# Block products for the remaining projection pairs of a hybrid encoder layer, with a shorter weight ring and the decay work rearranged

## The chip, the cores and the metric

The kernel runs on one core of one Trainium2 chip, as one launch. The metric is the device time in microseconds (us). Three runs of the kernel before took 1218.38, 1219.05 and 1219.12 us, median 1219.05.

## The reference

One encoder layer on 256 tokens of width 1024, all in float32 (products by leading sizes):

```python
def token_mixer(h, ...):
    proj = h @ w_in                                   # (256,1024) @ (1024, 6176)
    z, xbc, dt_f, dt_b, q, k, v, gates = jnp.split(proj, SPLITS, axis=-1)
    xbc = jax.nn.silu(depthwise_conv(xbc, conv_w, conv_b))
    dtf, dtb = softplus(dt_f + dt_bias_f), softplus(dt_b + dt_bias_b)
    y = y_f + y_b + xs * d_skip                       # two SSD scans, 16 heads of 64, 2 groups
    y = rmsnorm(y * jax.nn.silu(z), g_ssm)
    br_ssm = y @ w_br_ssm
    q, k = rope(rmsnorm(q)), rope(rmsnorm(k))         # 8 query heads, 2 key/value heads of 128
    br_attn = blocked_attention(q, k, v) @ w_br_attn
    g_s, g_a = jnp.split(jax.nn.sigmoid(gates), 2, axis=-1)
    return (g_s * br_ssm + g_a * br_attn) @ w_out

x = x + token_mixer(rmsnorm(x, g_mix), ...)
x = x + moe_ffn(rmsnorm(x, g_ffn), ...)               # top 4 of 32 experts, each 1024x2048 and 1024x1024
return rmsnorm(x, g_final)
```

In the scan a head's weight for output token l and input token s is exp(a_l - a_s) times dt_s times (C_l . B_s) for s <= l in the forward direction, and mirrored in the backward one, with a the running sum of dt times A.

## The kernel before, in words

The mixer reads its weights as 36 "units" of 1024 rows by 256 columns (1 MB each): 6 for x, B and C (U_XBC), 4 for z (U_Z), key (U_K), 4 query (U_Q), value (U_V), 8 gates (U_G), 4 of w_br_attn (U_BA), 4 of w_br_ssm (U_BS), 4 of w_out (U_O). They pass through a ring of `RING_MIX` = 10 slots of SBUF: SyncE (SP) loads unit n when unit n - 10 is done (`unit_done`), in order of n, and behind certain units stand the loads of the running sums for the decay (`load_seg`). The rest of the ring's space, `over`, holds other things of the mixer (gates, xbc, z, q and k). Afterwards the whole space is a ring of 8 pairs of slots for the experts' weights (402.7 MB in all), of which 22 MB can be loaded ahead. `PAIR_ORDER` and `first_free` say in which order these pairs come free.

On TensorE a unit is 16 products of 128x256 (each is two rows of the trace, float32). The four query units are done as two pairs in another way, `query_pair`: the two units are the halves of a 2x2 block matrix, the tokens and the inner dimension are halved too, and seven block products of four products each take the place of eight (Strassen's scheme in Winograd's form). VectorE makes the sums of weights (`pair_sum_t1` to `t4`, 128x1024 each) and of rows; ScalarE copies three partial sums out of PSUM (`pair_parts`); VectorE adds four quarters of the result. An output of such a pair has its tokens on the partitions; gate and branch units before the change have their channels on the partitions (`unit(n, rhs=...)`).

The loop `for g in range(8)` is the head stage. Group g is two scan heads and one attention head: TensorE does gate unit g, the transposes of the attention weights (L716), the scores of head g+1 (L700), the scan's product (L729) and the attention output (L739). VectorE makes the masked exponents of the decay (`seg_mask`), the maxima of the scores, the scan's output and its gate by z (L1655, L1658), the softmax's scaling (L1637, L1639) and the weights (`seg_weight`, which multiplies by dt and by C.B). ScalarE takes the exponentials. Each engine works through its own queue in the order written; semaphores join the queues. Behind the head stage come the branch units, the sum of the two gated branches, w_out, the router, and then 32 experts, which read the stream of weights.

Of the kernel before, what the change touches and what calls it, by code (L numbers as in the profile page):

```python
# [40 lines left out]
PICKED = -2e38  # L41

UW = 256
UNIT = KD * UW
RING_MIX = 10
# [3 lines left out]
PAIR_ORDER = (7, 3, 4, 0, 6, 5, 1, 2)  # L49
# [10 lines left out]
U_XBC, U_Z, U_K, U_Q, U_V, U_G, U_BA, U_BS, U_O = 0, 6, 10, 11, 15, 16, 24, 28, 32  # L60
N_MIX = 36

# [40 lines left out]
def encoder_layer(nc, x, g_mix, w_in, conv_w, conv_b, dt_bias_f, dt_bias_b, a_log_f, a_log_b, d_skip,  # L103
                  g_ssm, q_norm_g, k_norm_g, w_br_ssm, w_br_attn, w_out, g_ffn, w_router, b_router,
                  w_mlp1, b_mlp1, w_mlp2, b_mlp2, g_final, consts, out):
    with ExitStack() as ctx:
# [15 lines left out]
        def sem(name):  # L122
# [6 lines left out]
        over = sb("over", [P, (RING - RING_MIX) * UNIT], at=place_of["ring"] + RING_MIX * UNIT * 4)  # L129
        sig = over[:, 0:4096].rearrange("p (m l) -> p m l", m=16)  # L130
        roped = over[:, 0:2560].rearrange("p (t n) -> p t n", t=TT)
# [3 lines left out]
        qk = over[:, 9216:11776].rearrange("p (t n) -> p t n", t=TT)  # L135
        kT = over[:, 11776:12288].rearrange("p (h l) -> p h l", h=KVH)

# [23 lines left out]
        stat = sb("stat", [P, 64])  # L161

# [3 lines left out]
        rB = arena[:, 2048:2304]  # L166
# [6 lines left out]
        ebuf = arena[:, 4880:6416].rearrange("p (h l) -> p h l", h=2)  # L173
        ropeb = arena[:, 4880:5392].rearrange("p (t n) -> p t n", t=TT)
        gbuf = arena[:, 6416:8464].rearrange("p (b h i l) -> p b h i l", b=2, h=2, i=TT)
        sum_a = [a.rearrange("p (k l) -> p k l", k=KD // 2) for a in
                 (arena[:, 5392:5904], arena[:, 5904:6416], arena[:, 8976:9488], arena[:, 8464:8976])]
        sum_w = [[a.rearrange("p (k l) -> p k l", k=KD // 2) for a in part] for part in
                 ((arena[:, 0:1024], arena[:, 1024:2048], arena[:, 6416:7440]),
                  (arena[:, 7440:8464], arena[:, 1024:2048], arena[:, 6416:7440]))]  # L180
        part_a, part_b = rB, sqb
# [54 lines left out]
        def x_quarter(t, half):  # L236
            return hT[:, half * (KD // 2):(half + 1) * (KD // 2), t * P:(t + 1) * P]
# [15 lines left out]
        act_step = sem("act_step"); dve_step = sem("dve_step"); pool_step = sem("pool_step")  # L253
# [12 lines left out]
        sums_ready = sem("sums_ready"); prod_psum = sem("prod_psum"); first_taken = sem("first_taken"); quarter_ready = sem("quarter_ready")  # L266
        qsq_ready = sem("qsq_ready"); qr_ready = sem("qr_ready"); roped_ready = sem("roped_ready")
        qT_psum = sem("qT_psum"); qT_ready = sem("qT_ready")
        seg_masked = sem("seg_masked"); seg_exp = sem("seg_exp"); g_ready = sem("g_ready")
# [5 lines left out]
        yr_ready = sem("yr_ready"); rB_psum = sem("rB_psum")  # L275
        ssq_psum = sem("ssq_psum"); ssq_ready = sem("ssq_ready"); rB_ready = sem("rB_ready")
# [59 lines left out]
        def mix_src(n):  # L336
# [6 lines left out]
            if n < U_V:  # L343
                return cols(w_in[0], Q0 + (n - U_Q) * UW)
            if n == U_V:
                return cols(w_in[0], Q0 + AH * AD + KVH * AD)
            if n < U_BA:
                return cols(w_in[0], G0 + (n - U_G) * UW)
# [64 lines left out]
        def _(sp):  # L413
# [12 lines left out]
            for n in range(N_MIX):  # L426
# [7 lines left out]
                if U_G + RING_MIX <= n < U_G + RING_MIX + 6:  # L434
                    g = n - U_G - RING_MIX + 2
                    sp.wait_ge(seg_masked, 2 * g - 2)
                    if g == 3:
                        sp.wait_ge(roped_ready, 5)
                    load_seg(g)

            def first_free(p):
                if 2 * p < RING_MIX:
                    sp.wait_ge(unit_done, max(n for n in range(N_MIX) if mix_slot(n) == 2 * p + 1) + 1)
                elif p == 7:
                    sp.wait_ge(sc_psum, AH)
                    sp.wait_ge(roped_ready, 5)
                    sp.wait_ge(seg_masked, NH)
                    sp.wait_ge(yz_ready, 2 * KD)
                elif p == 6:
                    sp.wait_ge(cb_psum, 2)  # L450
                    sp.wait_ge(yz_ready, 2 * KD)
                    sp.wait_ge(unit_done, U_O)
                    sp.wait_ge(yg_ready, KD)
                else:
                    sp.wait_ge(mix_ready, 4)
# [1456 lines left out]
```

## Time and profile before

| | us |
|---|---|
| median of three runs | 1219.05 |
| profiled execution: its span, first to last instruction | 1218.8 |
| TensorE busy in it | 1178.1 |
| VectorE busy | 375.4 |
| ScalarE busy | 194.2 |
| GpSimd busy | 23.3 |

The times of the runs and the span of the profiled execution differ by 0.25 us; what lies around the span is within that. The page gives one execution: busy times, the span in 40 slices, and the chain that ended last. The rows further down are lines of that page and of the trace. Neighbouring instructions of one engine overlap a little in the trace (the end of one is recorded after the next has begun), so that the distance between two starts says what an instruction costs in a full queue, and its duration what it costs when someone waits for its end.

### The profile page before, as it was taken

Reading aid. Unit: us, or ns where it says so; the run is one execution under the profiler, and the core shown is the slowest. Engines: PE = TensorE matmul, PEld = TensorE weight load, DVE = VectorE, ACT = ScalarE, POOL = GpSimd, SP = SyncE. Lnnn points to the kernel's source line nnn. Section 1 sums busy time; section 2 is a strip of 40 time slices with the busy share of each in tenths; the row PEclk is TensorE's granted clock in tenths of the full one; section 3 lists DMA queues with packets and bytes.
Section 4 is the critical chain, followed back from the end, with each engine's and each line's share of the span. In section 5 each row is a group of like instructions: output and inputs, shape, how many; then the busy total and the mean of one; then the engine's idle time right before and its main releaser. Section 6 shows DMA issues by size and latency. Waiting matters only on the chain.

```text
span 1218.8 us, 14634 instructions
## 1 busy us (share of the span) xinstructions
PE 1178.1 (97%) x5561; PEld 561.1 (46%) x5561; DVE 375.4 (31%) x1034; ACT 194.2 (16%) x404; POOL 23.3 (2%) x36
## 2 busy tenths in 40 slices
PE   8999999999999999999999999999999999999996
PEld 7888888887433333333333333333333333333332
DVE  4537997122322222322222222222222222222212
ACT  2122344001111111111111111111111111111112
POOL 0001111000000000000000000000000000000000
PEclk9999999999999999999999999999999999999998
DMA  9945543667899999999999999999999999999995
GB/s 306 330 138 156 170 152 133 262 251 296 322 423 427 428 429 428 427 429 425 429 428 427 429 429 430 426 429 429 429 429 426 429 429 429 427 428 427 429 426 240
DMA packets 71479, 448.98 MB, mean 368 GB/s; under 512 B 6536, under 2 KB 44044, under 8 KB 45837
## 3 DMA queue, kind: packets, MB, share of 16 engines
q1 hardware_dynamic: 68186, 446.85, 89.5%
q10 hardware_dynamic: 3251, 1.54, 0.5%
q8 instruction: 30, 0.49, 0.2%
q14 instruction: 12, 0.10, 0.0%
HBM read 447.29 MB, written 1.08 MB: 368 GB/s over the span
## 4 chain that ended last, share of the span: by engine, by line
PE 76%; DMA 20%; ACT 2%; DVE 1%; issue 1%; POOL 0%; ACTq 0%; SPq 0%; DVEq 0%
PE bank L898 41%; DMA ring<-in_w_mlp_dram 19%; PE bank L580 14%; PE bank L893 4%; PE bank L873 4%; PE bank L583 2%; PE bank L882 1%; PE bank L937 1%; ACT arena L1319 1%; PE bank L644 1%; PE bank L729 1%; PE bank L556 1%; PE bank L887 1%; PE bank L739 1%; PE bank L805 1%
## 5 line engine op out<-in xcount | busy, mean ns | idle before, releaser
L898 PE MATMUL bank<-ring,arena 128*64 128x512 f32 x2928 | 654.8, 595 | 20.4 <-DMA ring<-in_w_mlp_dram 19.8
L898 PEld LDWEIGHTS bank<-ring,arena 128*64 128x64 f32 x2928 | 202.0, 137 | 417.4 <-issue 372.2
L1813 DVE TENSOR_TENSOR arena<-bank,b1T 128x256 f32<-128x256 f32 x126 | 53.1, 421 | 467.0 <-PE bank L937 463.9
L580 PE MATMUL bank<-hT,ring 128*128 128x256 f32 x544 | 119.6, 379 | 0.0
L580 PEld LDWEIGHTS bank<-hT,ring 128*128 128x128 f32 x544 | 103.1, 190 | 14.3 <-issue 0.4
L1316 ACT ACTIVATE arena<-bank 128x512 f32<-128x512 f32 x32 | 19.1, 597 | 404.9 <-PE bank L898 404.9
L1799 DVE TENSOR_TENSOR arena<-bank,prmT 128x512 f32<-128x512 f32 x30 | 20.8, 692 | 181.7 <-PE bank L882 181.7
L893 PE MATMUL bank<-arena 64*128 64x512 f32 x256 | 63.6, 615 | 0.8 <-ACT arena L1366 0.8
L873 PE MATMUL bank<-xres,arena 128*64 128x512 f32 x248 | 60.0, 604 | 0.0
L937 PE MATMUL bank<-cst,arena 128*128 128x128 f32 x256 | 42.0, 286 | 6.3 <-ACT arena L1319 6.3
L937 PEld LDWEIGHTS bank<-cst,arena 128*128 128x128 f32 x256 | 26.8, 140 | 39.9 <-ACT arena L1316 26.0
L1326 ACT ACTIVATE arena<-arena 128x256 f32<-128x256 f32 x64 | 26.7, 417 | 89.4 <-DVE arena L1815 89.4
L1349 ACT ACTIVATE arena<-bank 128x512 f32<-128x512 f32 x30 | 17.9, 597 | 123.6 <-PE bank L898 123.6
L873 PEld LDWEIGHTS bank<-xres,arena 128*64 128x64 f32 x248 | 15.1, 136 | 40.4 <-issue 40.4
L893 PEld LDWEIGHTS bank<-arena 64*128 64x128 f32 x256 | 22.0, 186 | 23.2 <-issue 21.6
L882 PEld LDWEIGHTS bank<-cst,arena 128*128 128x128 f32 x124 | 17.2, 207 | 25.2 <-issue 25.2
L583 PE MATMUL bank<-ring,hT 128*128 128x256 f32 x128 | 28.3, 379 | 0.0
L580 PE MATMUL bank<-arena,ring 128*128 128x256 f32 x128 | 28.2, 380 | 0.0
L580 PE MATMUL bank<-over,ring 128*128 128x256 f32 x128 | 27.8, 379 | 0.0
L1818 DVE SCALAR_TENSOR_TENSOR arena<-arena 128x256 f32<-128x256 f32 x62 | 26.4, 425 | 2.1
L1820 DVE TENSOR_TENSOR arena<-arena 128x256 f32<-128x256 f32 x62 | 26.3, 425 | 2.1
L1347 ACT ACTIVATE arena<-bank 128x256 f32<-128x256 f32 x30 | 11.5, 384 | 95.1 <-PE bank L887 95.1
(268 smaller groups left out, 803.7 us busy)
## 6 DMA issues: line engine op xcount, KB each, us to landing
ring<-in_w_mlp_dram SPq DMA_DIRECT2D x184, 2048.0 KB, 29.5
ring<-in_w_in_dram SPq DMA_DIRECT2D x24, 1024.0 KB, 11.4
ring<-in_w_mlp_dram SPq DMA_DIRECT2D x10, 1024.0 KB, 28.9
ring<-in_w_br_attn_dram SPq DMA_DIRECT2D x4, 1024.0 KB, 5.1
ring<-in_w_br_ssm_dram SPq DMA_DIRECT2D x4, 1024.0 KB, 5.2
ring<-in_w_out_dram SPq DMA_DIRECT2D x4, 1024.0 KB, 5.2
arena<-in_w_mlp_dram SPq DMA_DIRECT2D x3, 1024.0 KB, 13.0
arena<-acs_rows SPq DMA_DIRECT2D x4, 512.0 KB, 6.0
```

The costliest lines, as they stand in the source:

```text
L580: last = nc.tensor.matmul(o, w[:, k, a * P:(a + 1) * P], rhs[:, k, :], start=(k == 0), stop=(k == KD - 1))
L583: last = nc.tensor.matmul(o, tokens[:, k, a * P:(a + 1) * P], w[:, k, :], start=(k == 0), stop=(k == KD - 1))
L873: last = nc.tensor.matmul(bank[b][side * CAP:(side + 1) * CAP, :], slotG[:, par, t, :], xres[:, t, side * 512:(side + 1) * 512], start=(t ...
L882: last = nc.tensor.transpose(bank[b][:, m * P:(m + 1) * P], xrow[:, o + m % 2:o + UW:2], ident)
L893: return nc.tensor.matmul(bank[SUMS + q][:, :], wT_[rows, (q // 2) * P:(q // 2 + 1) * P], ysb[rows, :], start=False, stop=stop, skip_group ...
L898: return nc.tensor.matmul(bank[b][side * CAP:(side + 1) * CAP, :], tokens, w, start=start, stop=stop, skip_group_check=True)
L937: last = nc.tensor.transpose(bank[up + b][:, j * P:(j + 1) * P], hs[:, b * 512 + j * P:b * 512 + (j + 1) * P], ident)
L1326: nc.scalar.activation(sg.rearrange("p (i a s) -> p i a s", i=4, a=2)[:, :, h, :], ga.rearrange("p (i a s) -> p i a s", i=4, a=2)[:, :, h, ...
L1799: return V.tensor_tensor(x32.rearrange("p (d m) s -> p m d s", d=2), bank[b][:, :].rearrange("p (m d s) -> p m d s", m=4, d=2), prmT[:, R_ ...
L1813: step(V.tensor_tensor(o, side(bank[up + b][:, :]), bias_h.to_broadcast([P, 4, CAP]), ALU.add))
L1818: step(V.scalar_tensor_tensor(u_, u_, 1.0, g_, ALU.add, ALU.mult))
L1820: V.tensor_tensor(u_, u_, s_, ALU.mult).then_inc(actT_ready, 1)
```

## The change

Nine more pairs are done with seven block products: key with value (`P_KV`), four pairs of gates (`P_G` to `P_G + 3`), two of w_br_attn, two of w_br_ssm. The value unit moves from place 15 to 11. `query_pair` becomes `pair_step(p, step)`, whose seven steps are interleaved with the attention and scan heads (`heads(g)`), two heads to a pair. The ring for the mixer's units has 6 slots; the four slots behind it (`spare`) hold the sums and partial results. Gates and branches now have tokens on the partitions; their merged rows are turned by 16 transposes (`mix_transposes`) ahead of w_out, in place of the broadcast of the norm factor by a product (L753).

The decay work is put together in another way. ScalarE makes, by Relu with the running sum as its bias, the capped exponents of both heads (`decay_rows`, 8 instructions to a group), and one Exp over 1536 columns (`decays`); ln dt is part of the bias, so that VectorE no longer multiplies by dt; `decay_weights` is four instructions to a group in place of ten, and the mask is in C.B. The sums of squares and the scaling of q and k move to ScalarE; their gain goes into the cos and sin tables. One buffer holds the decays of a group: `decay_rows(g + 1)` waits for `decay_weights(g)` (`g_ready`).

Constants, ScalarE's decay work and VectorE's:

```diff
-RING_MIX = 10
+RING_MIX = 6
+SPARE = 4
-PAIR_ORDER = (7, 3, 4, 0, 6, 5, 1, 2)
+PAIR_ORDER = (7, 6, 0, 3, 4, 5, 1, 2)
...
+            def decay_rows(g, hh):
+                if hh == 0:
+                    act.wait_ge(seg_in[g % 2], 16 * (g // 2 + 1))
+                    act.wait_ge(acsN_ready, 2)
+                    if g >= 1:
+                        act.wait_ge(g_ready, g)
...
+                def below(o, rows, t, d):
+                    return nc.scalar.activation(o, rows, ACT.Relu, scale=-1.0, bias=nacs[:, t, d * NH + h:d * NH + h + 1])
+                below(decay[:, hh, 0, :], b[:, 0:256], 0, 0)
+                below(decay[:, hh, 1, :], b[:, 256:512], 1, 1)
+                below(decay_diag[:, hh, 0, :], b[:, 256:384], 0, 1)
+                below(decay_diag[:, hh, 1, :], b[:, 128:256], 1, 0).then_inc(seg_taken, 1)
+            def decays(g):
+                act.wait_ge(seg_taken, 2 * g + 2)
+                nc.scalar.activation(decay_all, decay_all, ACT.Exp, scale=-1.0, bias=ceil).then_inc(seg_exp, 1)
...
+            def decay_weights(g):
+                if g >= 2:
+                    dve.wait_ge(y_psum, g - 1)
+                dve.wait_ge(seg_exp, g + 1)
+                o = gbuf[:, g % 2, :, :, :]
+                k = g // (NH // 4)
+                V.tensor_tensor(o, decay, cb[:, k, :, :].unsqueeze(1).to_broadcast([P, 2, TT, 256]), ALU.mult)
+                link(V.tensor_tensor(decay_diag, decay_diag, cb_diag[k].unsqueeze(1).to_broadcast([P, 2, TT, P]), ALU.mult))
+                for i in range(TT):
+                    on = o[:, :, i, i * P:(i + 1) * P]
+                    last = V.tensor_tensor(on, on, decay_diag[:, :, i, :], ALU.add)
+                last.then_inc(g_ready, 1)
```

TensorE's order in the second and third gate pair (the first and the fourth are written out likewise):

```diff
+            for j in (1, 2):
+                pair_steps(P_G + j, 1, 2)
+                if j == 1:
+                    qk_transposes(3)
+                pair_steps(P_G + j, 3, 4)
+                heads(2 * j)
+                pair_steps(P_G + j, 5, 5)
+                if j == 1:
+                    qk_transposes(4)
+                pair_steps(P_G + j, 6, 7)
+                heads(2 * j + 1)
```

ScalarE's order there:

```diff
+            for j in (1, 2):
+                p = P_G + j
+                score_exps(2 * j)
+                first_part(p)
+                gate(j - 1)
+                y_square(2 * j - 1)
+                if j == 1:
+                    qT_copy(3)
+                decay_rows(2 * j + 1, 0)
+                second_part(p)
+                probT_copy(2 * j)
+                decay_rows(2 * j + 1, 1)
+                decays(2 * j + 1)
+                o_copy(2 * j)
+                score_exps(2 * j + 1)
+                third_part(p)
...
+                y_square(2 * j)
+                decay_rows(2 * j + 2, 0)
+                probT_copy(2 * j + 1)
+                decay_rows(2 * j + 2, 1)
+                decays(2 * j + 2)
+                o_copy(2 * j + 1)
```

VectorE's order there:

```diff
+            for j in (1, 2):
+                p = P_G + j
+                score_max(2 * j)
+                y_out(2 * j - 1)
+                weight_sum(p, 3)
+                quarter(p, 1)
+                prob_norm(2 * j)
+                if j == 1:
+                    rope(4)
+                weight_sum(p, 4)
+                decay_weights(2 * j + 1)
+                weight_sum(p + 1, 1)
+                score_max(2 * j + 1)
+                y_out(2 * j)
+                quarter(p, 2)
+                prob_norm(2 * j + 1)
+                quarter(p, 3)
+                quarter(p, 4)
+                decay_weights(2 * j + 2)
+                weight_sum(p + 1, 2)
```

VectorE in the head stage before: one whole group, from the maxima of the scores (L1632) to the weights of the next two heads (L1624 to L1628).

```order
L1632 TENSOR_REDUCE stat<-bank 128x2 [waits sc_psum]
L1633 TENSOR_SCALAR stat<-stat 128x2 [waits dve_step]
L1655 SCALAR_TENSOR_TENSOR over<-over,prmT,bank 128x256 [waits y_psum]
L1658 TENSOR_TENSOR over<-over 128x256 [waits yz_ready]
L1637 RECIPROCAL stat<-stat 128x2 [waits sc_exp]
L1639 TENSOR_SCALAR arena<-arena,stat 128x256 [waits dve_step]
L1639 TENSOR_SCALAR arena<-arena,stat 128x256
L1624 TENSOR_SCALAR arena<-arena,dtv 128x256 [waits seg_exp,y_psum]
L1625 TENSOR_SCALAR arena<-arena,dtv 128x256
```

Behind these stand eight more instructions of weights and the eight of the next `seg_mask`. VectorE in the change, second half of a pair in the head stage; L1835 to L1839 are `decay_weights`, L1687 a `weight_sum`, L1844 `score_max`, L1856 `y_out`, L1755 `quarter`.

```order
L1835 TENSOR_TENSOR arena<-arena 128x1024 [waits seg_exp,y_psum]
L1836 TENSOR_TENSOR arena<-arena,cst 128x512
L1839 TENSOR_TENSOR arena<-arena 128x2x128 [waits dve_step]
L1839 TENSOR_TENSOR arena<-arena 128x2x128
L1687 TENSOR_TENSOR spare<-ring 128x1024 [waits prod_psum,slot_full5,slot_full4]
L1844 TENSOR_REDUCE stat<-bank 128x2 [waits sc_psum]
L1845 TENSOR_SCALAR stat<-stat 128x2 [waits dve_step]
L1856 SCALAR_TENSOR_TENSOR over<-over,prmT,bank 128x256 [waits y_psum]
L1859 TENSOR_TENSOR over<-over 128x256 [waits yz_ready]
L1755 TENSOR_TENSOR spare<-spare,bank 128x256 [waits unit_taken]
```

The masks are gone from this queue, and the next maxima stand behind the instruction that waits for ScalarE's Exp (`seg_exp`). ScalarE before, one group: scores' Exp (L1255), decay's Exp (L1248), copy of the output, square and gain, tanh of the gate (L1266), copy of the transposes.

```order
L1255 ACTIVATE arena,stat<-bank,stat 128x256 [waits probT_psum,sc_max]
L1255 ACTIVATE arena,stat<-bank,stat 128x256
L1248 ACTIVATE arena<-arena 128x768 [waits seg_masked] x2
L1276 ACTIVATE arena<-bank 128x256 [waits o_psum]
L1281 ACTIVATE arena<-over 128x256 [waits ysq_added,yz_ready]
L1282 ACTIVATE over<-over,prmT 128x256
L1266 ACTIVATE over<-bank 128x512 [waits unit_done]
L1271 ACTIVATE arena<-bank 128x512 [waits o_psum,probT_psum]
```

ScalarE in the change, first half of a pair: scores' Exp (L1341), `first_part` (L1273), `gate` (L1367), `y_square`, `decay_rows` (L1324), `second_part` (L1280), `probT_copy` (L1350), `decays` (L1334).

```order
L1341 ACTIVATE arena,stat<-bank,stat 128x256 [waits probT_psum,sc_max]
L1341 ACTIVATE arena,stat<-bank,stat 128x256
L1273 ACTIVATE spare<-bank 128x256 [waits quarter_ready,prod_psum]
L1367 ACTIVATE over<-over 128x1024 [waits quarter_ready]
L1360 ACTIVATE arena<-over 128x256 [waits ysq_added,yz_ready]
L1361 ACTIVATE over<-over,prmT 128x256
L1324 ACTIVATE arena<-over,nacs 128x256 [waits g_ready,acsN_ready,seg_in1]
L1324 ACTIVATE arena<-over,nacs 128x256
L1324 ACTIVATE arena<-over,nacs 128x128 x2
L1280 ACTIVATE spare<-bank 128x256 [waits quarter_ready,prod_psum]
L1350 ACTIVATE arena<-bank 128x512 [waits o_psum,probT_psum]
L1324 ACTIVATE arena<-over,nacs 128x256 x2
```

Behind them stand two more `decay_rows` of 128 columns and `decays`, the Exp over 1536. All of these are now behind the scores' Exp, which waits for VectorE's maxima (`sc_max`).

## Rows read from the trace of the kernel before

**Rows 1.** The page: what DMA moved in each of 40 slices.

```profile
GB/s 306 330 138 156 170 152 133 262 251 296 322 423 427 428 429 428 427 429 425 429 428 427 429 429 430 426 429 429 429 429 426 429 429 429 427 428 427 429 426 240
```

**Rows 2.** Whom TensorE waited for: us in total, times, longest.

```profile
PE bank L898 <- DMA ring<-in_w_mlp_dram: 20.0, 24, 1.3
```

**Rows 3.** Chain that ended last, in order of time: start us, us, what.

```profile
95.39 12.20 PE bank L644 x56
...
141.34 6.91 PE bank L580 x32
148.25 0.44 PE bank L716 x4
...
149.56 1.02 PE bank L729 x8
150.57 1.06 PE bank L739 x4
...
212.51 6.91 PE bank L580 x32
...
268.65 6.91 PE bank L769 x32
```

**Rows 4.** Stretches: length, busy us of each engine, granted clock, DMA.

```profile
11.00:12.00 1.00, 1.00 (x5) 0.80 (x4) 1.00 (x4) 0.00 (x0) 0.00 (x0) 0.57 1.10 347
160.00:180.00 20.00, 20.00 (x103) 16.60 (x100) 19.02 (x53) 8.84 (x22) 2.45 (x2) 1.00 0.45 156
```

**Rows 5.** VectorE's groups by form, 0 to 310 us: busy, mean ns | idle.

```profile
L1488 DVE TENSOR_TENSOR arena<-ring,arena 128x1024 f32<-128x1024 f32 x2 | 2.4, 1221 | 0.0
L1562 DVE TENSOR_TENSOR over<-arena,bank 128x256 f32<-128x256 f32 x8 | 3.3, 418 | 4.2 <-PE bank L644 2.7 <-ACT arena L1220 1.5
```

**Rows 6.** VectorE in order of time, 160 to 172.5 us: start, us, what.

```profile
161.02 0.68 DVE L1632 TENSOR_REDUCE stat<-bank 128x2 f32<-128x512 f32 x1
...
162.32 0.42 DVE L1658 TENSOR_TENSOR over<-over 128x256 f32<-128x256 f32 x1
162.99 0.17 DVE L1637 RECIPROCAL stat<-stat 128x2 f32<-128x2 f32 x1 [0.25 <-ACT arena L1255]
163.19 0.62 DVE L1639 TENSOR_SCALAR arena<-arena,stat 128x256 f32<-128x256 f32 x2
...
167.47 0.69 DVE L1628 TENSOR_TENSOR arena<-arena 128x512 f32<-128x512 f32 x1
```

**Rows 7.** ScalarE in order of time, 160 to 183 us.

```profile
161.94 0.47 ACT L1255 ACTIVATE arena<-bank,stat 128x256 f32<-128x256 f32 x1 [2.27 <-DVE stat L1633]
...
162.85 1.57 ACT L1248 ACTIVATE arena<-arena 128x768 f32<-128x768 f32 x2
164.32 0.38 ACT L1276 ACTIVATE arena<-bank 128x256 f32<-128x256 f32 x1
164.58 0.42 ACT L1281 ACTIVATE arena<-over 128x256 f32<-128x256 f32 x1
164.89 0.51 ACT L1282 ACTIVATE over<-over,prmT 128x256 f32<-128x256 f32 x1
...
169.37 0.59 ACT L1271 ACTIVATE arena<-bank 128x512 f32<-128x512 f32 x1
```

**Rows 8.** ScalarE in order of time, 87 to 125 us: a table load.

```profile
87.88 1.28 ACT L1193 ACT_TABLE_LOAD   x1
```

**Rows 9.** TensorE in order of time, 0 to 20 us.

```profile
8.58 0.30 PE L540 MATMUL bank<-cst,prm 96*128 96x96 f32 x1 [1.27 <-DMA prm<-in_conv_w_dram]
...
10.64 8.83 PE L556 MATMUL bank<-hT,ring 128*128 128x256 f32 x32 [0.73 <-DVE hT L1455]
```

**Rows 10.** SyncE's transfers in order of time, 100 to 420 us.

```profile
199.74 27.44 SPq L429 DMA_DIRECT2D ring<-in_w_out_dram  x4
227.27 0.53 SPq L463 DMA_DIRECT2D mix_only<-in_w_mlp_dram  x1
...
309.52 2.08 SPq L484 DMA_DIRECT2D ring<-in_w_mlp_dram  x2
```

More of the change, by code:

```diff
@@ L670, in _, with product @@
-            query_pair(0)
-            pe.wait_ge(acsN_ready, 2)
-            for t in range(TT):
-                last = nc.tensor.transpose(bank[7][0:32, 256 + t * P:256 + (t + 1) * P], acsN[:, t, :], ident)
-            last.then_inc(acsT_psum, 1)
+            def product(o, a, w, start=True):
+                for k in range(KD // 2):
+                    last = nc.tensor.matmul(o, a[:, k, :], w[:, k, :], start=(start and k == 0), stop=(k == KD // 2 - 1),
+                                            skip_group_check=True)
+                return last
@@ L702, in scores, with heads @@
                 last.then_inc(sc_psum, 1)
[L704 to L709 removed]
+            def heads(g):
                 pe.wait_ge(prob_ready, g + 1)
@@ new lines, in _, with out_half @@
+            pair_steps(P_BS + 1, 1, 3)
+            mix_transposes(0)
+            pair_steps(P_BS + 1, 4, 7)
+            def out_half(n, h):
+                w = k_view(mix_slot(n))
+                for a in range(2):
+                    for k in range(h * (KD // 2), (h + 1) * (KD // 2)):
+                        last = nc.tensor.matmul(bank[n % 2][:, a * 256:(a + 1) * 256], hT[:, k, a * P:(a + 1) * P], w[:, k, :],
+                                                start=(k == 0 and a == 0), stop=(k == KD - 1), skip_group_check=True)
+                return last
@@ new lines, in _ @@
+            p = P_G + 3
+            score_exps(6)
+            first_part(p)
+            gate(2)
+            y_square(5)
+            decay_rows(7, 0)
+            second_part(p)
+            probT_copy(6)
+            decay_rows(7, 1)
+            decays(7)
+            o_copy(6)
+            score_exps(7)
+            y_square(6)
+            third_part(p)
+            probT_copy(7)
+            o_copy(7)
+            y_square(7)
+            first_part(P_BA)
+            gate(3)
+            second_part(P_BA)
@@ L1507, in _ @@
+            quarter(P_KV, 1)
             dve.wait_ge(dt_exp, 2)
@@ new lines, in _ @@
+            decay_weights(0)
+            quarter(P_Q + 1, 4)
+            weight_sum(P_G, 4)
+            score_max(0)
+            rope(2)
+            quarter(P_G, 1)
+            prob_norm(0)
+            decay_weights(1)
+            rope(3)
+            score_max(1)
+            y_out(0)
+            quarter(P_G, 2)
+            prob_norm(1)
+            quarter(P_G, 3)
+            quarter(P_G, 4)
+            weight_sum(P_G + 1, 1)
+            weight_sum(P_G + 1, 2)
+            decay_weights(2)
@@ new lines, in _ @@
+            p = P_G + 3
+            score_max(6)
+            y_out(5)
+            weight_sum(p, 3)
+            quarter(p, 1)
+            prob_norm(6)
+            weight_sum(p, 4)
+            decay_weights(7)
+            score_max(7)
+            y_out(6)
+            quarter(p, 2)
+            prob_norm(7)
+            weight_sum(P_BA, 1)
+            weight_sum(P_BA, 2)
+            y_out(7)
+            quarter(p, 3)
+            dve.wait_ge(o_ready, 8)
+            row_sum(P_BA, 1)
+            row_sum(P_BA, 2)
```

762 lines of the change are left out of this document (447 added, 315 removed).

## The prediction, written before the changed kernel ran

> **What bounds the kernel now.** I began with who waits for whom. TensorE waits 20.0 us for the experts' weights, in 24 waits [rows 2], and hardly for anything else. So there are two regimes. In the experts' part DMA moves some 428 GB/s in every slice from the twelfth on [rows 1], and the stream of weights sets the end; in the mixer the chain runs through TensorE product after product [rows 3]. A gate group is one unit, 6.91 us for 32 rows or 0.216 us a row, then transposes 0.44, scores 0.87 (the gap up to 149.56), scan product 1.02 and attention output 1.06: 10.3 us without a hole [rows 3]. In the same stretch VectorE is busy 19.0 of 20 us and ScalarE 8.8 [rows 4]. TensorE is the bound, VectorE stands close behind it. What shortens the mixer moves the first expert, and with it the release of ring slots and the whole stream, by the same amount.
>
> **The change, TensorE's work.** A pair in block products leaves out one product in eight: 8 of 64 rows, 8 x 0.216 = 1.73 us. Nine pairs: -15.5. The merged rows need 16 transposes, four times the 0.44 for four [rows 3]: +1.75. The broadcast of the norm factor goes, two rows: -0.43. Together -14.2 us, if nothing waits. The two pairs of queries were block products before (12.20 us for 56 rows [rows 3]) and give nothing.
>
> **VectorE's work in a gate pair.** Added: four weight sums at 1.14 (the row of 1.22 less the overlap of neighbours) and four quarters at 0.34 (0.42 alone) [rows 5], 5.9 us. `decay_weights` for one group is 1024 columns 1.14, 512 with a wait for its end 0.72 [rows 6], two of 256 at 0.34 and 0.42: 2.6. Maxima 0.9 (161.02 to ScalarE's start at 161.94 [rows 6, 7]), scan output 0.9, scaling 0.8 (162.99 to 163.81 [rows 6]) stay. Pair: 5.9 + 2 x (2.6 + 0.9 + 0.9 + 0.8) = 16.3, with some thirty handovers at 0.04 about 17.5, where TensorE has 12.1 + 2 x 3.4 = 18.9 us of work. By the sum of work the change fits. The masks of C.B (eight of 128 columns, 2 us) and the tables of cos and sin (1.2) stand beside query products, and a rope loses its sum and its scaling; I cost these at nothing.
>
> **ScalarE's work in a gate pair.** Instructions in a full queue: PSUM copy of 256 columns 0.26, square 0.31, scaling by a column 0.41 (0.51 less 0.1), copy of 512 0.50; two scores' Exps with sums 0.91 [rows 7]. No row is a Relu with a column as bias. From below it is the square without such an operand, 0.31 for 256 and 0.20 for 128 columns (768 take 0.73 [rows 7], 0.83 ns more per column); from above the scaling with one, 0.41 and 0.30, which has the same operands. I take the upper one: a head 2 x 0.41 + 2 x 0.30 = 1.42, the lower would be 1.02. Exp over 1536 columns: 0.84 for 768 [half of rows 7's 1.57, with its end], plus 768 x 0.83 ns and 0.1 for the bias column: 1.56. Tanh over 1024: 0.31 + 768 x 0.83 ns = 0.95. A pair has two each of Exps 0.91, output copy 0.26, square and gain 0.72, rows 2.84, transposes 0.50, Exp 1.47, and tanh and three parts at 0.26: 15.1 us. This fits too.
>
> The Trainium skill, "ScalarE: Activation LUTs", What ACT_TABLE_LOAD costs, gives for a column as bias 280 ns + 0.833 ns per column and an overlap of 93 ns; by it a head would take 1.39, so that the sum would be 0.5 us lower in eight groups, and the row with a column operand (0.51) agrees. Its Rules for kernel authors say to keep relu on VectorE, against this change; the reason given there is speed per element, mine is the order below.
>
> **The ring of waits.** The sums say nothing of order. There is one decay buffer: `decay_rows(g+1)` needs `decay_weights(g)`. ScalarE's queue has the scores' Exp ahead of these rows, and that Exp needs the maxima, which stand on VectorE behind `decay_weights(g)` and a weight sum; the next `decay_weights` stands ahead of everything else on VectorE until ScalarE's Exp is done. So the two engines work by turns. First half of a pair, counted from the end of `decay_weights(2j)`: weight sum 1.14, maxima 0.9, scores' Exp 0.95, first part 0.26, tanh 0.95, square and gain 0.72, rows 1.42, second part 0.26, copy of transposes 0.50, rows 1.42, their end 0.1, Exp 1.6, `decay_weights` 2.62: 12.8. TensorE adds a wait: it needs the first part (at 3.4) before its third step, 1.73 + 1.73 + 0.44 later the transposes are there, at 7.4, while ScalarE was ready at 6.6. Half: 13.6. Second half: 1.14 + 0.9 + 0.95 + third part 0.26 + 0.72 + 1.42 = 5.4; but the third part (3.3) frees quarter 2 on VectorE (3.8), that the seventh step, and that the transposes, at 6.15. From there copy 0.55, rows 1.42, 0.1, Exp 1.6, `decay_weights` 2.62: 12.4. A pair takes 26.0 us against 18.9 of TensorE's work and 20.6 for two groups before.
>
> TensorE so waits in the third step for `first_part`, 3.4 us, and in the seventh for quarter 2, 3.7. Pairs two and three: 6.8 and 7.2 (the second has transposes of 0.44 more). Last pair by the same walk: 3.4, then 4.9 for the scaling of head 7: 8.5. First pair: ScalarE's queue there also holds 16 short instructions for sums of squares and scaling, and two table loads (1.28 each [rows 8]) ahead of the first Exp. Carrying the three queues forward, scores' scaling of head 0 comes 3.9 us after TensorE asks, and the seventh step waits 6.0, as two ropes of 2.25 and `decay_weights(1)` precede quarter 2. Sum of the new waits 9.9 + 6.8 + 7.2 + 8.5 = 32.4. The kernel before had waits of its own here: from 95.39 to 212.51 are 117.1 us [rows 3] for 115.9 of products, so 1.2 go. Net +31.2.
>
> In the branch pairs nothing queues: VectorE has 4 x 0.85 + 4 x 1.14 = 8 us (11 with the factor's second step and row sums) under 12.1 of products, and the turned rows are behind steps four to seven.
>
> **The clock.** Between 8.58 and 10.64 and just ahead TensorE idles 1.27 and 0.73 us [rows 9]; in the stretch from 11 the granted clock is 0.57 [rows 4], on its way to the lower level, 1.2 GHz, and the next 32 rows take 8.83 instead of 6.91 us: 1.9 for one fall. The eight new waits are 3 to 6 us each, longer than these. Below: 0, when the slow stretch lies in the wait. Above: 8 x 1.9 = 15.4. I take six falls with half their price, 5.8, since part of a slow stretch falls on products that are not on the ring.
>
> "TensorE: Matmul & The Clock Gate", Part 1, of the Trainium skill says that idling lowers the clock and sustained work raises it; the start of this trace agrees, no row shows it for a gap within steady work.
>
> **SyncE's queue.** With six slots unit 35 is issued when unit 29 is done, at the end of the first w_br_ssm pair, 13 us before the branch units end; before it was issued in the 27 us from 199.74, and the experts' stream began at 227.27 [rows 10]. Now 2 + 22 MB, 56 us at 428 GB/s, have 13 + 40.9 + 0.9 = 55 us up to the first release (268.65 to 309.52 in the old kernel [rows 3, 10]). DMA has no rest there, where the old kernel had 82 us (227.27 to 309.52 [rows 10]) for 22 MB, 51 us' worth. Loss 0 to 3, I take 0. `load_seg` holds unit loads back until decay rows are taken, but each still lands a pair ahead.
>
> **Sum.** -14.2 + 31.2 + 5.8 = +22.8. On the execution's 1218.8 us that is 1241.6; the median is 0.25 us above the span, and I predict 1242.
>
> **Rivals.**
> 1. *Faster: the ring never closes.* If ScalarE and VectorE run ahead far enough, TensorE stays the bound, as both sums of work (17.5 and 15.1) allow: 1219.05 - 14.2 = 1204.8. It decides when the waits, clock included, drop below 15.4 us of my 38.2, so from a ring of about 22 us a pair down. Against it: the order of the queues, which I cannot make overlap. Chance 0.15.
> 2. *A shorter ring.* Relu at the lower bound saves 0.8 a group, 6.4 in eight, and no clock falls: 1242 - 6.4 - 5.8 = 1230. Chance 0.16.
> 3. *Every fall at full price*: 1242 + 9.6 = 1251.5. Chance 0.12.
> 4. *The weights come late*: the last ring slots are filled after the first release; +3, 1245. For it the missing slack, against it a stream that has no rest. Chance 0.03.
>
> **Chances.** The forecast itself, 1236 to 1247, has 0.49; 0.05 remain for a result within 0.2% of before (about what a measurement can tell from no change), between rival 1 and 2. Faster 0.15, same 0.05, slower 0.80. The range 1210 to 1254 leaves out most of rival 1's centre and the tail of rival 3; for slower cases alone it is 1226 to 1254.
>
> **What would show it.** VectorE idle ahead of L1835, released by ScalarE's L1334, some 4 us each, and ScalarE idle ahead of L1341, released by L1845; TensorE idle at L650 behind L1273 and L1755, 30 us in all; starts of gate pairs 26 us apart; the granted clock below 1 in the head stage; the first expert product near 330 instead of 307.5; a branch pair in 12.1 us. It would be wrong if the gate pairs start 19 to 21 us apart, or if the experts' part is longer or shorter than before by more than 2 us.

## The result, and the profile after

The changed kernel takes 1242.3 us (median of four, 1241.9 to 1244.9), the kernel before 1218.8 (four runs, 1218.4 to 1219.1). The ratio is 1.0195, 95% interval 1.0181 to 1.0209, so 23.5 us or 1.9% more. The forecast was 1242, slower.

The profiled run took 1242.42 us with a span of 1240.6 us. The span grew by 21.8 us and the median by 23.5; the difference lies in the two profiled executions, and the start shows it. This is TensorE in the changed kernel (start, duration, engine, line, operation, tiles, shapes, count, idle time before and its releaser):

```profile
10.81 7.14 PE L579 MATMUL bank<-hT,ring 128*128 128x256 f32 x32 [0.72 <-DVE hT L1652]
```

The same 32 rows took 8.83 us in the profiled run of before [rows 9]: that run was 1.7 us slower at the very start. Its granted clock was 0.50 from 12 to 14 us, where the changed kernel's was 1.00 behind a wait of the same length. It goes with the execution and not with the kernel: later profiles of changed kernels show 7.14 or 8.8 as well.

First, who waits for whom, in the stretch from 120 to 245 us (total us, times, longest), on TensorE, then VectorE, then ScalarE:

```profile
PE bank L650 <- DVE over L1755: 11.2, 4, 4.0
PE bank L650 <- ACT spare L1273: 7.2, 3, 2.9
PE bank L723 <- DVE arena L1851: 6.3, 2, 3.2
...
DVE arena L1835 <- ACT arena L1334: 30.6, 8, 5.7
...
ACT arena L1341 <- DVE stat L1845: 31.6, 8, 4.4
```

The kernel before has no TensorE wait there. Now TensorE waits 24.6 us: 11.2 for quarters, 7.2 for `first_part`, 6.3 for scaled scores. VectorE and ScalarE wait for each other in turn, 3.8 and 4.0 us on average in each of eight groups: the ring.

One turn of it, on ScalarE and then VectorE:

```profile
167.80 1.58 ACT L1334 ACTIVATE arena<-arena,stat 128x1536 f32<-128x1536 f32 x1
169.28 0.36 ACT L1354 ACTIVATE arena<-bank 128x256 f32<-128x256 f32 x1
174.06 0.47 ACT L1341 ACTIVATE arena<-bank,stat 128x256 f32<-128x256 f32 x1 [4.42 <-DVE stat L1845]
```

```profile
169.47 1.23 DVE L1835 TENSOR_TENSOR arena<-arena 128x1024 f32<-128x1024 f32 x1 [2.48 <-ACT arena L1334]
170.62 0.68 DVE L1836 TENSOR_TENSOR arena<-arena 128x512 f32<-128x512 f32 x1
171.33 0.76 DVE L1839 TENSOR_TENSOR arena<-arena 128x256 f32<-128x256 f32 x2
172.01 1.22 DVE L1687 TENSOR_TENSOR spare<-ring 128x1024 f32<-128x1024 f32 x1
173.15 0.68 DVE L1844 TENSOR_REDUCE stat<-bank 128x2 f32<-128x512 f32 x1
173.86 0.17 DVE L1845 TENSOR_SCALAR stat<-stat 128x2 f32<-128x2 f32 x1
```

VectorE stands still until ScalarE's Exp of the decays ends at 169.4; then ScalarE stands still from 169.6 to 174.06, while VectorE multiplies the decays (L1835 to L1839), makes a weight sum (L1687) and only then takes the maxima (L1844). TensorE in the same pair and the next:

```profile
161.62 3.69 PE L650 MATMUL bank<-spare 128*128 128x256 f32 x16 [1.61 <-ACT spare L1273]
...
175.87 2.60 PE L650 MATMUL bank<-ring,spare 128*128 128x256 f32 x8 [3.27 <-DVE over L1755]
178.26 1.06 PE L723 MATMUL bank<-cst,arena 128*128 128x128 f32 x4
179.11 1.73 PE L712 MATMUL bank<-over,arena 128*128 128x256 f32 x4
...
182.76 3.62 PE L650 MATMUL bank<-ring,hT 128*128 128x256 f32 x16
```

After the wait of 3.27 us eight rows take 2.60 us instead of 1.89, transposes 1.06 instead of 0.60 and scores 1.73 instead of 1.03. The granted clock says why (stretch; busy time and count of TensorE, its weight loads, VectorE, ScalarE and GpSimd; clock; DMA):

```profile
145.00:150.00 5.00, 1.63 (x4) 1.36 (x5) 3.72 (x11) 3.43 (x11) 0.90 (x1) 0.64 0.71 211
150.00:155.00 5.00, 5.00 (x23) 3.48 (x21) 2.70 (x3) 2.37 (x7) 0.00 (x0) 0.68 0.32 75
...
160.00:165.00 5.00, 3.39 (x17) 3.02 (x17) 4.93 (x13) 4.81 (x14) 0.90 (x1) 1.00 0.01 3
...
175.00:180.00 5.00, 4.13 (x15) 3.46 (x16) 1.86 (x6) 3.56 (x11) 0.83 (x1) 0.71 0.45 152
```

The clock is on its way to or at the lower level, 1.2 GHz, behind the waits of 4.00 and 3.27 us, and at the upper behind the one of 1.61. There are six such stretches in the head stage. The length of a wait does not settle it alone: at the same place, in the run with the held stream below, the eight rows behind a wait of 3.28 us take 1.99 us, close to the 1.89 of full rate:

```profile
175.13 1.99 PE L651 MATMUL bank<-ring,spare 128*128 128x256 f32 x8 [3.28 <-DVE over L1756]
```

From the first step of the first gate pair (123.79) to the first branch pair (238.03) are 114.2 us. The work in it is 76.7: four pairs of 12.1, eight groups of 3.38, three sets of transposes of 0.44. Idle time is 24.6, and 12.9 us are left. Of these 11.1 are products at the lower clock: each of the six stretches, up to the first product at full rate, is 1.6 to 2.5 us longer than the same products elsewhere, 1.85 on average. The other 1.8 stand at the edges of the waits, where the clock is 1.00: the last product ahead of a wait is recorded to its end, 0.16 us beyond the distance at which the next would have started (1.89 us for eight rows against 1.73), and the first rows behind it take up to 0.1 more.

Behind the head stage, the first output unit, the first product of an expert, and GB/s in the 40 slices:

```profile
287.70 3.62 PE L834 MATMUL bank<-ring,hT 128*128 128x256 f32 x16
...
327.88 3.65 PE L976 MATMUL bank<-ring,arena 128*64 128x512 f32 x16 [0.58 <-DVE arena L2058]
```

```profile
GB/s 309 181 136 176 144 140 85 69 186 426 411 428 428 427 428 426 428 428 427 428 427 428 428 428 428 428 429 428 428 431 427 427 430 427 429 428 427 428 427 230
```

Before, the first expert product stood at 307.48, so it comes 20.4 us later (22.1 with the 1.7 of the start). The branch pairs have no wait. From the first expert product to the end are 912.7 us; before it was 911.3. In the eighth slice, where before moved 262 GB/s [rows 1], it is 69: the stream of the experts has not begun.

### The profile page after: what moved, and what is told of

It is laid out like the page before. It is cut to its first block, busy times and chain, and to the rows that moved or that the text cites. A ratio compares the mean times of both kernels' runs of the same rounds, so it can differ in the third digit from the quotient of the medians.

```text
span 1240.6 us, 14746 instructions
## 1 busy us (share of the span) xinstructions
PE 1175.2 (95%) x5503; PEld 553.8 (45%) x5503; DVE 395.1 (32%) x1004; ACT 238.2 (19%) x542; POOL 22.0 (2%) x36
## 4 chain that ended last, share of the span: by engine, by line
PE 71%; DMA 19%; ACT 4%; DVE 3%; issue 1%; ACTq 0%; POOL 0%; SPq 0%; DVEq 0%
PE bank L976 40%; DMA ring<-in_w_mlp_dram 19%; PE bank L650 9%; PE bank L603 5%; PE bank L971 4%; PE bank L951 4%; PE bank L1015 1%; PE bank L960 1%; ACT arena L1515 1%; PE bank L834 1%; ACT arena L1334 1%; ACT arena L1324 1%; DVE arena L1835 1%; PE bank L965 1%; PE bank L884 1%
## 5 line engine op out<-in xcount | busy, mean ns | idle before, releaser
L603 PE MATMUL bank<-hT,ring 128*128 128x256 f32 x288 | 63.0, 380 | 0.0
L603 PEld LDWEIGHTS bank<-hT,ring 128*128 128x128 f32 x288 | 54.5, 190 | 7.7 <-issue 0.4
L650 PE MATMUL bank<-ring,spare 128*128 128x256 f32 x176 | 45.1, 402 | 11.0 <-DVE over L1755 11.0
L650 PE MATMUL bank<-spare 128*128 128x256 f32 x176 | 41.2, 384 | 7.3 <-ACT spare L1273 7.2
L1015 PEld LDWEIGHTS bank<-cst,arena 128*128 128x128 f32 x256 | 26.8, 140 | 39.9 <-ACT arena L1512 26.7
L650 PEld LDWEIGHTS bank<-ring,spare 128*128 128x128 f32 x176 | 34.7, 199 | 17.1 <-DVE over L1755 12.2
L650 PEld LDWEIGHTS bank<-spare 128*128 128x128 f32 x176 | 33.0, 191 | 12.9 <-issue 8.1
L951 PEld LDWEIGHTS bank<-xres,arena 128*64 128x64 f32 x248 | 15.1, 136 | 40.4 <-issue 40.4
L971 PEld LDWEIGHTS bank<-arena 64*128 64x128 f32 x256 | 22.0, 186 | 23.2 <-issue 21.6
```

The source lines that it names most:

```text
L603: last = nc.tensor.matmul(o, w[:, k, a * P:(a + 1) * P], rhs[:, k, :], start=(k == 0), stop=(k == KD - 1))
L650: last = nc.tensor.matmul(o, a[:, k, :], w[:, k, :], start=(start and k == 0), stop=(k == KD // 2 - 1), skip_group_check=True)
L951: last = nc.tensor.matmul(bank[b][side * CAP:(side + 1) * CAP, :], slotG[:, par, t, :], xres[:, t, side * 512:(side + 1) * 512], start=(t ...
L971: return nc.tensor.matmul(bank[SUMS + q][:, :], wT_[rows, (q // 2) * P:(q // 2 + 1) * P], ysb[rows, :], start=False, stop=stop, skip_group ...
L1015: last = nc.tensor.transpose(bank[up + b][:, j * P:(j + 1) * P], hs[:, b * 512 + j * P:b * 512 + (j + 1) * P], ident)
```

## Experiments

All are edits of the changed kernel. "Head stage" is the time from the first step of the first gate pair to the first branch pair.

**The maxima ahead of the decays.** On VectorE in every group:

```diff
                 weight_sum(p, 4)
+                score_max(2 * j + 1)
+                y_out(2 * j)
                 decay_weights(2 * j + 1)
                 weight_sum(p + 1, 1)
-                score_max(2 * j + 1)
-                y_out(2 * j)
```

> On VectorE, score_max and y_out stand ahead of decay_weights in every group instead of behind it; nothing else is changed. Ring theory (ScalarE and VectorE work by turns because the maxima stand behind decay_weights): from the end of decay_weights both engines go on at once, a pair of gate units falls from 27.5 us to about 19 to 21, most of the 24.6 us of TensorE's waits and of the 13.2 us of slow clock go: 1206 to 1216 us, first expert product near 300. One-buffer theory (the single decay buffer alone makes the engines alternate, the place of the maxima does not matter): at most 5 us less, 1237 or above. Theory of sums (VectorE has too much work in a pair): also at most a few us less, and VectorE busy throughout.

Measured: 1223.1 us (1220.4 to 1226.7), ratio to before 1.0028 (1.0016 to 1.0040). The order of two helpers is worth 19 us of the 23.5. The one-buffer theory (at most 5 us less) and the theory of sums (at most a few) fall. The ring theory had the direction and most of the size, but the result is 7 us above the end of its range. TensorE's waits show where they are:

```profile
PE bank L650 <- DVE over L1755: 6.4, 4, 2.7
PE bank L723 <- DVE arena L1851: 5.5, 3, 3.1
PE bank L650 <- issue: 2.4, 2, 1.2
```

14.3 us of idle time are left, 1.7 of slow clock in one stretch (behind the wait of 3.13 us) and 2.1 at the edges of the waits: head stage 94.8 (125.38 to 220.21). `decay_weights` still stands ahead of the quarter that step 7 wants, and the first pair, with ropes and sums of squares, still waits twice, 3.13 and 2.69 us. The interlocking had more than one link. What a second buffer for the decays would give was not tried.

**More work on ScalarE, inside the ring**, in `decay_rows` of every head:

```diff
+                below(spare[:, 7680 + 256 * hh:7808 + 256 * hh], b[:, 256:384], 0, 1)
+                below(spare[:, 7808 + 256 * hh:7936 + 256 * hh], b[:, 128:256], 1, 0)
                 below(decay_diag[:, hh, 0, :], b[:, 256:384], 0, 1)
```

> Two more Relus of 128 columns per head on ScalarE, into a scratch buffer, ahead of the two that are kept: about 1.2 us more ScalarE work in each group, 7 groups of which lie in the head stage. Ring theory: the work lies on the ring, +6 to +9 us. If VectorE's sum of work or the weights set the time: 0 to +2 us, as ScalarE waits 31.6 us for the maxima alone.

Measured: 1250.7 us, 8.4 more than the changed kernel, for eight groups of 1.2 us on an engine that is busy 66.8 of the head stage's 114.2 us in the changed kernel. The head stage grows from 114.2 to 124.7.

**More work on VectorE, outside the ring**, ahead of its wait for the decays:

```diff
+                if g >= 1:
+                    V.tensor_reduce(stat[:, 48 + g:49 + g], spare[:, 0:1024], AXX, ALU.max)
                 dve.wait_ge(seg_exp, g + 1)
```

> One more reduction of 1024 columns on VectorE right ahead of the wait for decays in each of seven groups, about 1.1 us each, 7.7 us in all. Ring theory: VectorE idles 3.8 us on average in just this place, so it costs 0 to +1 us. If VectorE's sum of work bounds the head stage: +7 to +8 us.

Measured: 1241.4 us, 0.9 less, which four runs can't tell from no change. Groups of VectorE from 125 to 245 us (count; busy us, mean ns; idle time before and its releaser):

```profile
L1837 DVE TENSOR_TENSOR arena<-arena 128x1024 f32<-128x1024 f32 x8 | 9.8, 1224 | 22.3 <-ACT arena L1334 22.3
L1833 DVE TENSOR_REDUCE stat<-spare 128x1 f32<-128x1024 f32 x7 | 8.5, 1210 | 0.0
```

8.5 us of new work vanish in the wait, which falls from 30.6 to 22.3. The two runs together say it: 1.2 us a group cost their length on the ring and nothing beside it, though VectorE (71.4 us of 114.2) and ScalarE (66.8) are busy alike in the head stage of the changed kernel.

**More work on TensorE, ahead of its waits**, to part idle time from clock. Step 2 twice, and likewise step 6 in pairs one to three and step 4 in pairs one and four:

```diff
+                    if P_G < p < P_BA:
+                        product(o_z, a_quarter(p, 0, 1), w_quarter(n, 1))
                     product(o_z, a_quarter(p, 0, 1), w_quarter(n, 1)).then_inc(prod_psum, 1)
```

> TensorE makes one product of each gate pair's waits twice, with the same operands and the same result: step 2 twice in pairs two to four (ahead of the wait in step 3), step 6 twice in pairs one to three (ahead of the wait in step 7), step 4 twice in pairs one and four (ahead of the waits for the scaled scores of heads 0 and 7). That is 8 x 1.73 = 13.8 us more work at full clock, each piece ahead of a wait of 1.6 to 4.0 us. Ring theory with a clock that falls behind idle stretches: the work fills waits and keeps the clock, the 13.2 us of slow clock shrink; result between 1236 and 1243, TensorE's waits in the head stage down from 24.6 us to about 12 or less. If TensorE's work bounds the stage: +13.8, 1256. If the slow clock has nothing to do with idling: waits down by 13.8, clock as before, time the same, 1242.

Measured: 1238.6 us (1238.0 to 1241.2): 13.8 us more work, 3.7 us less time. Of the 3.7 the head stage has 1.8 (114.2 to 112.4); the rest lies ahead of it and in the experts' part, within what profiles differ by. Idle time is 15.1 us, 76.7 + 13.8 are work, and 6.8 are left, where it was 12.9: two stretches of slow clock with 4.8 us instead of six with 11.1, and 2.0 at the edges of the waits. TensorE is not the bound, and the slow stretches vanish where the waits get short. Windows of this run:

```profile
145.00:150.00 5.00, 2.32 (x6) 1.87 (x7) 3.06 (x10) 3.85 (x12) 0.89 (x1) 0.71 0.65 208
150.00:155.00 5.00, 5.00 (x21) 3.29 (x19) 2.78 (x3) 2.61 (x6) 0.00 (x0) 0.61 0.46 123
170.00:175.00 5.00, 4.18 (x22) 3.34 (x20) 4.63 (x9) 1.07 (x5) 0.00 (x0) 1.00 0.04 16
175.00:180.00 5.00, 4.27 (x25) 3.12 (x25) 1.86 (x6) 4.58 (x13) 0.83 (x1) 1.00 0.88 269
```

Behind the wait that stayed long (3.87 us) it is still 0.71 and 0.61; from 175 on, where 0.71 was, it is 1.00, since the wait ahead fell from 3.27 to 1.55. "TensorE: Matmul & The Clock Gate" of the Trainium skill, Part 1, says that idling lowers the clock; these windows now show it for gaps within steady work.

**Plain products in the gate pairs**, block products in the other seven, maxima ahead. PE's part of the edit:

```diff
-            pair_steps(P_G, 1, 1)
+            for g in range(8):
+                gate_half(g, 0)
...
+                gate_half(g, 1)
+                heads(g)
```

> The four gate pairs are plain products again (two units of 6.91 us, the tanh straight from PSUM, no weight sums and no quarters there), and score_max and y_out stand ahead of decay_weights; all else is as in the changed kernel: block products for keys and values, queries and branches, rows turned late, Relus and one Exp on ScalarE, six slots. By the sum of TensorE's work: -15.5 + 6.9 + 1.75 - 0.43 = -7.3 us against before, 1211 to 1213, if the heads' work fits under 10.3 us per group. If the decay work on ScalarE with its single buffer closes a ring even so: 1220 or more. If the six slots or the missing slack of the expert stream cost something: some us above 1212 with TensorE's waits in the head stage near none.

Measured: 1223.4 us (1221.6 to 1224.2), 11 above the expectation. TensorE waited in nearly every group, most often like this:

```profile
162.33 1.13 PE L752 MATMUL bank<-arena 128*128 128x256 f32 x4 [1.41 <-ACT arena L1355]
```

L1355 is the copy of the transposed scores, which I had left behind the first half of the next group's Relus. So it was moved:

```diff
-                if g < 7:
-                    decay_rows(g + 1, 0)
                 probT_copy(g)
                 if g < 7:
+                    decay_rows(g + 1, 0)
                     decay_rows(g + 1, 1)
```

> As the kernel with plain gate products, but on ScalarE the copy of the transposed scores stands ahead of the Relus for the next group instead of between them. There TensorE waited 0.9 to 1.4 us in six of eight groups for that copy. If these waits are why it did not come out at -7.3 us: 6 to 7 us off, 1216 to 1218. If the work of TensorE alone does not shrink as counted, or the rest was lost behind the head stage: no change, 1223.

Measured: 1218.7 us (1217.4 to 1221.6), ratio 1.0001 (0.9992 to 1.0010). 4.7 us came off, less than the 6 to 7 expected: 5.9 us of waits are left in a head stage of 90.8. The count closes: -7.3 of work, -1.2 for the waits of before, +5.9 idle, +1.2 at the edges of the waits (the granted clock is 1.00 in the whole head stage here), +1.5 in the experts' part, together +0.1; measured -0.4. The count of TensorE's work is right; its saving is eaten elsewhere.

**Decays late, in all pairs.** The order of the three engines is set by when TensorE asks, and ropes and transposes move too; the core of it on VectorE, put together from the edit:

```diff
+                prob_norm(2 * j)
                 weight_sum(p, 3)
+                weight_sum(p, 4)
+                decay_weights(2 * j)
                 quarter(p, 1)
...
                 score_max(2 * j + 1)
                 y_out(2 * j)
+                prob_norm(2 * j + 1)
...
                 quarter(p, 2)
+                if j < 3:
+                    decay_weights(2 * j + 1)
```

> All nine pairs in block products, as in the changed kernel, but the order on VectorE and ScalarE set by when TensorE asks: score_max, y_out, prob_norm and the quarter that frees a step stand ahead of decay_weights, which comes just ahead of the scan product that reads it; Relus go ahead of the scores' Exp only as far as they do not hold it; rope(2) stands in VectorE's idle time ahead of the first decays, rope(3) and rope(4) and their transposes go one half pair later. Ring theory: no wait is left that the order made; 10 to 18 us off the kernel with the maxima ahead, 1206 to 1213. Sum-of-work theory: VectorE has 17.5 us a pair and two ropes of 2.25 besides in 18.9 us, so that it becomes the bound: 1214 to 1222.

Measured: 1213.1 us (1211.4 to 1214.0), ratio to before 0.9949 (0.9936 to 0.9963). It is faster than both kernels and stands between the two ranges, 1206 to 1213 of the ring theory and 1214 to 1222 of the sum of work. The first three pairs have 1.5 us of idle time in all, in the last pair 5.1 are left:

```profile
PE bank L736 <- DVE arena L1820: 4.2, 2, 2.7
PE bank L704 <- DVE over L1796: 1.4, 1, 1.4
PE bank L746 <- ACT arena L1349: 0.9, 1, 0.9
```

**The last pair's order** on TensorE, and the transposes of the last two query heads behind step 2 of the third pair (not shown):

```diff
-            pair_steps(P_G + 3, 1, 3)
+            pair_steps(P_G + 3, 1, 4)
             heads(6)
-            pair_steps(P_G + 3, 4, 5)
+            pair_steps(P_G + 3, 5, 6)
             heads(7)
-            pair_steps(P_G + 3, 6, 7)
+            pair_steps(P_G + 3, 7, 7)
```

> The kernel with the late decays, with its three remaining holes closed by order alone: in the last gate pair TensorE makes step 4 ahead of head 6 and step 6 ahead of head 7 (it waited 1.45, 0.90 and 2.70 us there for decay_weights(6) and (7) and ran behind at the lower clock for some 1.5), and the transposes of queries 6 and 7 stand behind step 2 instead of step 1 (1.38 us). Ring theory: 4 to 5 us off, 1208 to 1210. If VectorE's sum of work is the bound by now: the waits move elsewhere, 1212 to 1213.

Measured: 1211.6 us (1209.8 to 1212.3), ratio 0.9932 (0.9918 to 0.9946): the fastest version, 7.4 us under the kernel before. It gained 1.5 of the 4 to 5 us expected, which is nearer to what the sum of work foretold (1212 to 1213, the waits move). Part of the waits moved: 0.61 and 0.90 us appear at head 4, and the 2.70 at head 7 stays. Its cause was not tried further.

**VectorE's load on the opened ring.** The same reduction as above, on the kernel with the late decays:

> One more reduction of 1024 columns (1.21 us, 1.14 in a row with others) on VectorE ahead of each of seven waits for decays, as in the run on the changed kernel, but on top of the kernel with the late decays. There VectorE is busy 4.8 to 4.9 of 5 us in most of the head stage. If VectorE's sum of work is what bounds the head stage once the ring is open: +5 to +8 us, where the same edit cost nothing in the changed kernel. If the ring is still there: 0 to +2.

Measured: 1216.0 us (1214.2 to 1218.3), 2.9 more than without it. It lies between the two expectations: of some 8 us a third comes through, where in the changed kernel nothing did. VectorE is busy nearly throughout in several windows of the kernel with the late decays itself (third pair of numbers after the length):

```profile
160.00:165.00 5.00, 4.41 (x23) 2.89 (x21) 4.93 (x13) 3.97 (x13) 0.00 (x0) 1.00 1.04 345
165.00:170.00 5.00, 4.21 (x22) 3.78 (x23) 4.93 (x8) 4.39 (x9) 1.19 (x1) 1.00 0.34 122
170.00:175.00 5.00, 5.00 (x29) 3.71 (x28) 4.84 (x10) 3.41 (x10) 0.00 (x0) 1.00 0.01 3
```

VectorE has 4.84 to 4.93 us of 5 there, and 71.8 of 85.7 us in the whole head stage, so it is close to being the bound once the ring is open: both theories hold in part.

**The experts' stream held back.**

```diff
             sp.wait_ge(o_psum, AH)
+            sp.wait_ge(unit_done, U_O - 1)
             for u in AWAY_EARLY:
```

> The changed kernel with one more wait on SyncE: the experts' first loads go out after step 6 of the last branch pair instead of one pair earlier, at about 284 instead of 275.4 us. If the stream of weights has slack left in the changed kernel (the forecast's loss of 0): 0 to +2 us. If six slots already took the slack and the stream bounds the experts' part from its first load on: the whole delay of about 9 us, +7 to +9.

Measured: 1250.7 us (1249.4 to 1252.9), 8.4 more. The first loads went out at 286.45 instead of 275.40, 11 us later and not the 9 expected; the first expert product did not move (328.11), and from it to the end are 921.3 us instead of 912.7. TensorE's waits for weights:

```profile
PE bank L977 <- DMA ring<-in_w_mlp_dram: 27.8, 32, 1.3
```

They are 21.6 in 25 waits in the changed kernel and begin 448 us behind the first expert product there, 363 us behind it here. So 11.05 us of delay cost 8.6 in the experts' part. If what goes beyond the slack is paid in full, which one run can't show, the changed kernel has some 2.4 us of slack between the stream and the experts.

## Why the prediction was right

- **TensorE's work, -14.2.** Holds. A branch pair takes 12.1 us, and from the first branch pair to the first output unit are 49.7 us where before had 56.1 for eight units and their scan sums: -6.5, as 4 x 1.73 and 0.43 less 0.87 for the first transposes give. The runs with plain gate products close by the same count.
- **The ring of waits.** Holds in place and in cause: the three waits stand in the lines foretold, and moving the maxima takes 19 us away. Pairs start 26.8, 27.5 and 27.8 us apart behind the first, where 26.0 was forecast without the clock. The walk can be checked half by half, from the end of one `decay_weights` to the next (the one at 171.33 is shown above):

```profile
158.59 0.76 DVE L1839 TENSOR_TENSOR arena<-arena 128x256 f32<-128x256 f32 x2
...
184.90 0.76 DVE L1839 TENSOR_TENSOR arena<-arena 128x256 f32<-128x256 f32 x2
...
198.79 0.76 DVE L1839 TENSOR_TENSOR arena<-arena 128x256 f32<-128x256 f32 x2
...
212.51 0.76 DVE L1839 TENSOR_TENSOR arena<-arena 128x256 f32<-128x256 f32 x2
```

  First halves take 12.7 us, without the weight sum of 1.1 that stands elsewhere in that pair, and 13.9 (forecast 13.6), second halves 13.6 and 13.7 (forecast 12.4).
- **The clock, +5.8.** Holds as the addition that it was meant to be. Six falls were forecast and six are there, at 1.85 us each, 11.1 in all, close to the full price of 1.9. But not all of that lengthens the turn: the second halves are 1.2 and 1.3 us over the walk, and that is step 7 and the transposes at the lower clock, 3.49 us from 175.87 to ScalarE's copy at 179.36, where the walk had 2.35. The slow scores behind them only fill time in which TensorE would have waited. So idle time is 24.6 us and not 32.4, one of the signs that did not come out as written (30 us in all), and the sum of what is not work is 37.5, where the forecast had 32.4 + 5.8 = 38.2: if the walk's 32.4 is taken as it stands, the clock added 5.1. The run with steps made twice is in line with this (6.3 us less of slow clock, 1.8 less of head stage), but it adds work as well and can't part the shares. That six of eight waits would bring a fall was taken and not worked out; in that number there is luck.
- **ScalarE's prices.** The upper bound was right. The Exp over 1536 columns takes 1.57 to 1.58 us (forecast 1.56; its three terms add up to 1.58), and a head's four Relus, with the next instruction:

```profile
163.50 1.49 ACT L1324 ACTIVATE arena<-over,nacs 128x256 f32<-128x256 f32 x4
164.88 0.38 ACT L1280 ACTIVATE spare<-bank 128x256 f32<-128x256 f32 x1
```

  The next instruction starts 1.38 us behind the first of them; forecast 1.42. The section on What ACT_TABLE_LOAD costs in "ScalarE: Activation LUTs" of the Trainium skill made 1.39 of it, and the trace agrees.
- **SyncE's queue, 0.** Perhaps low: the experts' part is 1.4 us longer in the changed kernel than before (912.7 and 911.3), but it is 911.4 to 913.0 in the eight experiments up to the last pair's order, so that one profile of each can't tell 1.4 from their spread (it is 914.5 in the one with VectorE's added load on the late decays). The held stream shows little slack, some 2.4 us and not the 30 that the prediction counts for before. Its range of 0 to 3 held it. Rival 4's mechanism is possible and small here.
- **The base.** The 0.25 us between the median and the span was wrong: all later runs take 1.8 us more than their spans, so that the profiled execution of before took about 1220.6, 1.8 above the median of four, by its slow start. It did no harm, since span plus 0.25 is the median of the three runs, 1219.05, which is 0.3 above the median of four. With the measured terms the sum is 1218.8 - 14.2 - 1.2 + 37.5 + 1.4 = 1242.3. Against the forecast the base is 0.3 lower, the waits with the clock 0.7 lower, and the experts' part 1.4 higher. That these nearly cancel is luck.
- **Rivals.** Rival 1 was not out of reach by the sums of work, as I said: with another order on TensorE, VectorE and ScalarE the same work takes 1211.6. That is still 7 us above its 1204.8. Rival 3 had the price of a fall right and missed that part of it falls into time that is waited anyway.

## What to carry to other kernels

When two helpers each have slack by their sums, walk their queues once around: where one engine's next input stands behind the other's long operation, and the other's behind this one's, they work by turns, and neither busy share shows it. Put what another engine waits for ahead of what only a later step reads. Add a little work at a place to ask whether it lies on such a ring: here 1.2 us a group cost 8.4 us at one place and nothing at another. And a saving on the engine that was the bound is worth only what the next constraint leaves: here 14.2 us of products became 7.4 us after the queues had been put in order.

## What the runs showed of the hardware

A weight sum of VectorE over 1024 columns takes 1.22 us, and GpSimd's addition of 256 columns 0.72 (at 189.92 below). When they meet, both can take longer. From the run with the maxima ahead, VectorE and then GpSimd:

```profile
178.93 1.22 DVE L1692 TENSOR_TENSOR spare<-ring,spare 128x1024 f32<-128x1024 f32 x1
180.06 1.75 DVE L1694 TENSOR_TENSOR ring<-ring 128x1024 f32<-128x1024 f32 x1
```

```profile
179.16 1.57 POOL L1618 TENSOR_TENSOR arena<-arena 128x256 f32<-128x256 f32 x1 [10.39 <-ACT arena L1360]
189.92 0.72 POOL L1618 TENSOR_TENSOR arena<-arena 128x256 f32<-128x256 f32 x1 [9.19 <-ACT arena L1360]
```

"SBUF — State Buffer" of the Trainium skill, Who interferes with whom, says that a VectorE instruction with two inputs in SBUF contends with a GpSimd one that reads SBUF; these rows agree. GpSimd starts at 179.16 within VectorE's first instruction, which keeps its 1.22, and takes 1.57, 0.85 more than alone; VectorE's next instruction starts at 180.06, while GpSimd is still at work, and takes 1.75, 0.5 more.
